# One gate tile moved from the cache stage into the recurrence chain and its outputs, and eight key pages loaded before the cache stage

## The reference, cut to what matters

```python
xn = rms_norm(h); z = xn @ w_in
za, zb, ga, gb = z[..., :c1], z[..., c1:c2], z[..., c2:c3], z[..., c3:]
oa, s_new, _ = rwkv_branch(za, shift0, s0, p)   # a recurrence over time, 8 heads, state 64x64
q, k, v, log_f = fox_features(zb, ...)
ob = attend(q, k, v, log_f)                     # samples: over 2048 cached keys in 16 pages each
merged = sigmoid(ga) * (oa @ proj_a) + sigmoid(gb) * (ob @ proj_b)
h = h + merged @ w_out
h = h + hier_moe(rms_norm(h))                   # 32 experts, two of them for each token
y = rms_norm(h)
```

## Time and profile before

| | us |
|---|---|
| median of 3 runs | 859.84 |
| lowest and highest | 859.52, 865.72 |
| the profiled execution's own time | 862.67 |
| its span, first to last instruction | 861.0 |
| PE busy in the span | 761.1 (88%) |
| DVE busy | 382.5 (44%) |
| ACT busy | 186.4 (22%) |
| POOL busy | 145.3 (17%) |
| mean traffic of the transfers | 254 GB/s |

### The profile page before, as it was taken

The page is one execution under the profiler, slowest core; times in us unless marked ns, Lnnn a source line. Parts: engine busy times, 40 slices in busy tenths (PEclk is TensorE's granted clock), DMA queues, the critical chain, the costliest instruction groups (busy, mean ns, idle before and its releaser), DMA issues. The chain is left out here.

```text
span 861.0 us, 20782 instructions
## 1 busy us (share of the span) xinstructions
PE 761.1 (88%) x8681; PEld 445.5 (52%) x8681; DVE 382.5 (44%) x722; ACT 186.4 (22%) x433; POOL 145.3 (17%) x294
## 2 busy tenths in 40 slices
PE   5999999998989999768898997889889987899985
PEld 2445666675666667624565664455644425444421
DVE  2222623228963174748666774633552222422213
ACT  2101321216332210031422320223111110111103
POOL 8500120007020020031504343422000000000000
PEclk9999999988999989768899998999989998999997
DMA  8721431211332113459899999988939999999993
GB/s 311 284 86 54 190 117 49 97 53 67 103 85 84 32 55 85 105 163 396 364 352 414 397 397 409 362 313 314 422 153 425 421 425 421 426 420 425 421 412 121
DMA packets 54647, 220.26 MB, mean 256 GB/s; under 512 B 21935, under 2 KB 24026, under 8 KB 30746
## 3 DMA queue, kind: packets, MB, share of 16 engines
q1 hardware_dynamic: 46576, 183.28, 54.5%
q0 software_dynamic: 7328, 35.48, 10.7%
q10 hardware_dynamic: 650, 0.18, 0.1%
HBM read 211.82 MB, written 7.09 MB: 254 GB/s over the span
## 5 line engine op out<-in xcount | busy, mean ns | idle before, releaser
L232 PE MATMUL bank<-arena 128*128 128x320 f32 x256 | 85.0, 469 | 3.1 <-DVEq L2200 1.8
L208 POOL DMA_DIRECT2D arena<-in_cv x116 | 59.9, 516 | 113.1 <-PE bank L1897 80.8
L513 PE MATMUL bank<-arena 128*128 128x512 f32 (+1 forms) x144 | 69.9, 624 | 1.4 <-DMA arena<-in_w_zb 1.4
L2508 PE MATMUL bank<-arena 128*32 128x512 f32 x512 | 65.4, 624 | 3.3 <-DMA arena<-in_w_exp 2.1
L2739 DVE TENSOR_TENSOR arena<-arena,bank 128x512 f32<-128x512 f32 x35 | 24.1, 687 | 97.2 <-PE bank L2478 94.2
L548 PE MATMUL bank<-arena 128*128 128x336 f32 x224 | 66.3, 450 | 0.6 <-ACT arena L429 0.6
L1590 DVE STREAM_TRANSPOSE arena<-arena 128x2048 f32<-128x2048 f32 x28 | 63.1, 2288 | 4.3 <-DMA arena<-in_ck 2.9
L232 PEld LDWEIGHTS bank<-arena 128*128 128x128 f32 x256 | 47.5, 199 | 24.8 <-issue 7.6
L1897 PE MATMUL bank<-arena 128*16 128x128 f32 x1024 | 35.6, 300 | 19.7 <-issue 11.4
L548 PEld LDWEIGHTS bank<-arena 128*128 128x128 f32 x224 | 41.5, 189 | 21.4 <-issue 1.7
L1389 ACT ACTIVATE arena<-bank 128x384 f32<-128x384 f32 (+6 forms) x63 | 25.1, 444 | 108.2 <-PE bank L232 31.9
(11 more groups left out here) (495 smaller groups left out, 1103.4 us busy)
## 6 DMA issues: line engine op xcount, KB each, us to landing
arena<-in_w_exp SPq DMA_DIRECT2D x95, 1024.0 KB, 19.1
arena<-in_ck SPq DMA_DIRECT2D x120, 256.0 KB, 6.6
arena<-in_cv POOLq DMA_DIRECT2D x116, 256.0 KB, 7.6
arena<-in_w_gate SPq DMA_DIRECT2D x8, 1024.0 KB, 4.8
arena<-in_w_za SPq DMA_DIRECT2D x7, 1024.0 KB, 6.9
arena<-in_w_zb SPq DMA_DIRECT2D x6, 1024.0 KB, 15.7
arena<-in_w_proj SPq DMA_DIRECT2D x8, 512.0 KB, 9.9
arena<-in_w_out SPq DMA_DIRECT2D x4, 1024.0 KB, 10.6
```

Of the source, the lines that this page charges most:

```text
L208: eng.dma_start(tile[n:P:4, :], src[bass.ds(page, 1)].rearrange("a (p j) n -> (a p) (j n)", j=4))\
L232: mm = nc.tensor.matmul(bank[b][:, 0:TM], w[:, k, a, :], xnT[:, k, NMETA:T], start=(k == 0), stop=(k == KT - 1))
L513: mm = nc.tensor.matmul(bank[q % 6][0:n, :], xnT[:, k, i * P:i * P + n], w[:, k % 4, :], start=(k == 0), stop=(k == KT - 1))
L2508: mm = nc.tensor.matmul(bank[2][j * CAP:(j + 1) * CAP, :], xg[:, q % 2, k, j * CAP:(j + 1) * CAP], place[s][:, (k % 4) * 512:(k % 4 + 1) * ...
```

## The change

It concerns the end of "rwkv_pairs" and the start of "cache".

- `GT_PAIRS` goes from 14 to 15: tile 14 is made in "rwkv_pairs". Its first four slices come after the last two chain steps (`chain_gate` after each of the nine steps now), its last four between the groups of the outputs (after n = 1, 4, 7, 10). It uses bank 3, so the outputs go to banks 0, 1, 2 and 4, and PE waits for the copy of bank 4 first. Only tile 15 is left to "cache".
- SP issues the eight key pages of m = 0, 1 of sequence 1 in "rwkv_pairs", after the suffix sums (L1101) and ahead of the stores of tiles 12, 13 and 14. To make their place free, `cd` and `um` move behind them in memory, and `xl` into `ar`.
- The four transfers of the final state move from the end of "rwkv_pairs" to "cache", behind the projection loads, and with them goes SP's wait there for the stored tiles. The wait for them stands ahead of `key_loads(2)`, as before.
- In "cache" SP takes the four pages of m = 2 from POOL; POOL keeps m = 3.
- On DVE, `turn_keys(1, 0)` stands ahead of the wait for the variance, and `turn_keys(1, 1)` ahead of the reciprocal's wait instead of behind the reciprocal.

```diff
-        GT_PRE, GT_LEVELS, GT_SOLVE, GT_SAMPLES, GT_PAIRS = 6, 9, 11, 12, 14
+        GT_PRE, GT_LEVELS, GT_SOLVE, GT_SAMPLES, GT_PAIRS = 6, 9, 11, 12, 15
...
@@ rwkv_pairs, sync
+                for m in range(2):
+                    load_pages(sp, 11 + m, page_numbers(sp, m, 1), A["ck"])
                 gates_out(GT_SAMPLES, GT_PAIRS)
-                for i in range(2):
-                    sp.wait_ge(S(f"kept_gt{i}"), 16 * (GT_PAIRS // 2))
-                sp.wait_ge(S("w_sp_sb"), 1)
-                for g in range(NPAIR):
-                    sp.dma_start(O["rw_p"][2 * g:2 * g + 2].rearrange("h v k -> v h k"),
-                                 soutp[hs[g % 2], g // 2, :].rearrange("p (h k) -> p h k", h=2)).then_inc(S("kept_rw"), 16)
...
@@ rwkv_pairs, tensor
                     mm.then_inc(S("w_sp"), 1)
-                    if c < 7:
-                        chain_gate(c + 1)
-
+                    chain_gate(c + 1)
+
+                OUT_BANK = (0, 1, 2, 4)
                 pe.wait_ge(S("w_s"), NCH)
-                pe.wait_ge(S("w_gt_sb"), GT_PAIRS - GT_PRE)
+                pe.wait_ge(S("w_o1_sb"), 1)
                 for g in range(NPAIR):
                     for j in range(NT):
...
+                        if (g, j) == (NPAIR - 1, NT - 1):
+                            mm.then_inc(S("w_o"), 1)
+                        n = g * NT + j
+                        if n % 3 == 1:
+                            mm = gate_mm(pe, GT_PAIRS - 1, 3, (4 + n // 3,))
+                            if n // 3 == 3:
+                                mm.then_inc(S("w_gt"), 1)
...
@@ cache, sync
-                for m in range(2):
-                    load_pages(sp, key_slot(1, m), page_numbers(sp, m, 1), A["ck"])
+                for n, page in enumerate(page_numbers(sp, 2, 1)):
+                    page_load(sp, place[key_slot(1, 2)], n, A["ck"], page, S("kept_key2"))
                 proj_load(sp, 0, 0)
                 proj_load(sp, 0, 1)
+                for g in range(NPAIR):
+                    sp.dma_start(O["rw_p"][2 * g:2 * g + 2].rearrange("h v k -> v h k"),
+                                 soutp[hs[g % 2], g // 2, :].rearrange("p (h k) -> p h k", h=2)).then_inc(S("kept_rw"), 16)
                 sp.wait_ge(S("kept_rw"), 16 * NPAIR * (DB + 1))
                 sp.wait_ge(S("ov_ps"), 1)
                 proj_load(sp, 1, 0)
                 key_loads(2)
+                for i in range(2):
+                    sp.wait_ge(S(f"kept_gt{i}"), 16 * ((GT_PAIRS + 1 - i) // 2))
                 sp.wait_ge(S("p_gt_out"), 16 * NPOST)
                 gates_load(0)
...
@@ cache, vector
                 turn_bias(0)
+                turn_keys(1, 0)
                 dve.wait_ge(S("ov_ps"), 1)
                 TS(ovs, bank[7][:, 0:T], 1.0 / HD, GN_EPS, mult, add).then_inc(S("ov_ready"), 1)
-                turn_keys(1, 0)
+                turn_keys(1, 1)
                 dve.wait_ge(S("ort_ready"), 1)
                 nc.vector.reciprocal(ovs, ovs).then_inc(S("ov_rc"), 1)
-                turn_keys(1, 1)
```

More of the change, by code:

```diff
@@ L1039, in build @@
         nn = sp4(NPAIR, 2, NT, CH)
-        cd = sp4(NPAIR, 2, 2, NT, CH)
         mark_bv = sp4.at
@@ L1046, in build @@
         vmm = sv(2, 4, P)
+        assert sp4.at <= odd_at + 2 * SLOT
+        sp4.at = odd_at + 2 * SLOT
+        cd = sp4(NPAIR, 2, 2, NT, CH)
         um = sp4(NPAIR, NT, P)
+        assert sp4.at <= stage[0].offset
         fin = Space(arena, mark_qb, mark_nn)
         soutp = fin(2, P)
+        assert mark_nn > odd_at >= fin.at
         us = [us_a, fin(4, P)]
-        xl = fin(NPAIR, P)
+        xl = ar[:, BE, :, 0:P]
         snew = [Space(arena, mark_nn, mark_nn + DB * HD)(DB, HD), fin(DB, HD)]
@@ L1374, in _ @@
                             for i in range(4):
-                                mm_(bank[i][hs[h], g * 96 + j * CH:g * 96 + (j + 1) * CH], v_tm[strips[i], g, j, hs[h]],
+                                mm_(bank[OUT_BANK[i]][hs[h], g * 96 + j * CH:g * 96 + (j + 1) * CH], v_tm[strips[i], g, j, hs[h]],
                                     cd[strips[i], g, h, 1, j, :], start=True, stop=False)
                             for i in range(4):
-                                mm = mm_(bank[i][hs[h], g * 96 + j * CH:g * 96 + (j + 1) * CH], um[strips[i], g, j, hs[h]],
+                                mm = mm_(bank[OUT_BANK[i]][hs[h], g * 96 + j * CH:g * 96 + (j + 1) * CH], um[strips[i], g, j, hs[h]],
                                          cd[strips[i], g, h, 0, j, :], start=False, stop=True)
-                mm.then_inc(S("w_o"), 1)
-                pe.wait_ge(S("w_o1_sb"), 1)
+                        if (g, j) == (NPAIR - 1, NT - 1):
[5 more added lines that the diff above has]
+                                mm.then_inc(S("w_gt"), 1)
+                pe.wait_ge(S("w_o1_sb"), 2)
                 for q in range(2):
-                    mm = nc.tensor.transpose(bank[4][:, q * P:(q + 1) * P],
+                    mm = nc.tensor.transpose(bank[5][:, q * P:(q + 1) * P],
                                              sbd[:, 2 * q:2 * q + 2, :].rearrange("p g v -> p (g v)"), ident)
@@ L1446, in _ @@
                 gate_out(GT_SOLVE, 7)
-                for j in range(GT_SAMPLES, GT_PAIRS):
-                    gate_out(j, 3)
+                gate_out(GT_SAMPLES, 3)
+                gate_out(GT_SAMPLES + 1, 3)
                 act.wait_ge(S("w_or"), NCH)
@@ L1451, in _ @@
                     cp(ar[:, AL, g, 0:LP], bank[4 + g][:, P:P + LP]).then_inc(S("w_o1_sb"), 1)
+                gate_out(GT_PAIRS - 1, 3)
                 act.wait_ge(S("w_sp_ps"), 1)
-                cp(soutp.rearrange("p q t -> p (q t)"), bank[4][:, 0:2 * P]).then_inc(S("w_sp_sb"), 1)
+                cp(soutp.rearrange("p q t -> p (q t)"), bank[5][:, 0:2 * P]).then_inc(S("w_sp_sb"), 1)
             @block.vector
@@ L1549, in _ @@
                 for i in range(4):
-                    ch(TT(ov[:, :, i, :], ov[:, :, i, :], bank[i][:, 0:384].rearrange("p (a c) -> p a c", c=CH), add))
+                    ch(TT(ov[:, :, i, :], ov[:, :, i, :], bank[(0, 1, 2, 4)[i]][:, 0:384].rearrange("p (a c) -> p a c", c=CH), add))
         retire()
@@ L1783, in _ @@
                 pool.sem_inc(S("hsel_ready"), 1)
[L1784 to L1787, removed]
+                pages = page_numbers(pool, 3, 1)
+                for i in range(2):
+                    pool.wait_ge(S(f"kept_gt{i}"), 16 * ((GT_PAIRS + 1 - i) // 2))
+                for n in range(4):
+                    page_load(nc.gpsimd, place[key_slot(1, 3)], n, A["ck"], pages[n], S("kept_key3"))
                 for g in range(NPAIR):
```

## The result

The changed kernel is slower. In 20 runs its median is 868.18 us (861.72 to 876.96), that of the kernel before, run beside it, 864.1 (854.08 to 878.6). The ratio is **1.0068, interval 1.0037 to 1.0099**: 5.9 us lost by 865, where the forecast was 8.0 won. The profiled execution took 868.66 us, its span is 867.1: 6.0 more than the profile of before. Disturbed executions, more than 1.5% above the fastest of the same kernel, are left out of the ratios and the readings, and the profiles of changed_again, changed_gates_early and before_again were such.

A forecast was written before the change was run, and what follows sets the result against it. PE, DVE and ACT handing work on in series, transfers close behind, were taken to bound the kernel; 0 (block start) + 8.0 (first fills earlier) = 8.0 won, 859.84 - 8.0 = 851.8 us, range 848 to 858.

The forecast's parts named there:

- Chain's end and outputs: End of the recurrence block: added gate slices leave the cache block's start unchanged, from 1 earlier to 4 us later.
- the term of 0.5: Outputs: four gate slices cost 0.5 us, mostly covered by PE's 3.6 us wait for issue; ends 0 and 5.6.
- DVE at the head: Cache block's head: earlier key turns start the maxima 4.2 us earlier and let `scores(1)` meet its keys 7.3 earlier.
- SP, with the moved stores: Cache block: state stores issued by 384.4 land 5 us later; `key_loads(2)` begins 1.5 late at 392.4, ends +0 and +19.
- The gates' landing: Cache block: gates' load issued at 406.7 instead of 410.76, the sigmoid beginning 5 to 6.6 us after it.
- the gap at 410 to 415: Cache block: idle transfer time there, 1.6 us, closes and counts toward transfers being about 7 us ahead.
- Sigmoid to `scores(2)`: Cache block: exponentials 3.76 us after the sigmoid, DVE takes fill output 3.9 later, then three fills at 2.6 each.
- one for one: Whole kernel: what is won before 630 us comes out at the end in full.
- the slower side: Rival, cache block: SP stands at state stores landing in 10.1 to 23.2 us, delaying keys, gates and fills; chance 0.07.
- Only the transfers count: Rival, whole cache block: only saved transfers matter, 3.5 to 5 us won, 855 to 856; chance 0.17.
- the outputs pay: Rival, outputs: four slices lie bare at the low clock, 5.6 us, block starts 4 later, 856; chance 0.11.
- the change does not do what it says: Rival: pages asked for in the chain block land only in the cache block; about 3 us won, 857; chance 0.04.

The follow-up runs named there:

- changed_again: The changed kernel run a second time, nothing altered, against the kernel before: ratio 1.0066 (1.0031 to 1.0102).
- changed_gates_early: The changed kernel, stores where the change puts them, with the first gates' load issued behind the pages of m = 1 of `key_loads(2)`: ratio to before 0.9959 (0.9925 to 0.9993).
- before_again: The kernel before, unchanged, timed against itself: ratio 0.9983 (0.9946 to 1.002).
- tile_alone: The kernel before with only the gate tile's move (tile 14 in the last chain steps and outputs): ratio to before 1.0002 (0.9972 to 1.0032).
- changed_third: The changed kernel run a third time, nothing altered, against the kernel before: ratio 1.0028 (0.998 to 1.0076).
- stores_first: The changed kernel with the four state stores as SP's first transfers of the cache block: ratio to before 0.9936, and 0.9933 the second time.
- stores_back: The changed kernel with the four state stores back at the end of "rwkv_pairs", behind the tiles' stores: ratio to before 0.994 (0.9906 to 0.9975).
- keys_ahead_of_wait: The changed kernel with `key_loads(2)` issued ahead of SP's wait for the state stores: ratio to before 0.9985 (0.9953 to 1.0017).
- stores_alone: The kernel before with only the state stores moved behind `proj_load(sp, 0, 1)`, and SP's wait for the state gone: ratio to before 1.0041 (1.0006 to 1.0076).

## Why the prediction was wrong

In the profile the changed kernel was 14.0 us from the forecast (8.0 won forecast, 6.0 lost). Two steps failed: SP's stand at the moved stores, and the landing time of the gates' load behind it. By its own steps:

- **Ahead of the change**, 2.6: chance, as shown. It is part of this profile, not of the 1.0068.
- **Chain's end and outputs**, taken at 0 with ends -1 and 4: 2.6 in this profile, 0.6 behind the eighth step, as forecast, and 2.0 from the ninth step to the block. Over ten profiles with the tile in the outputs, these take 11.3 to 13.7 us (mean 12.6), in three without it 10.5, 10.6 and 11.4. The group rows of the changed kernel (355 to 378 us) show why:

```profile
L232 PE MATMUL bank<-arena 128*128 128x320 f32 x16 | 6.5, 513 | 0.0
L1375 PE MATMUL bank<-arena 32*64 32x32 f32 x192 | 5.2, 238 | 4.3 <-issue 4.3
```

  The sixteen are four after the eighth step, four after the ninth (1.34 us each four) and eight in the outputs: 6.5 - 2 x 1.34 = 3.8 us for those. The wait for issue did not close over them as I argued: it was 4.3 us here, against 3.6 before, and 1.8 in tile_alone, where it closed in part. By the means, the term of 0.5 was too small by 1.2 and within its ends.
- **DVE at the head**: right. Maxima at +17.0 after the first matmul, +17.9 forecast; tile 15 done at +21.2, +23.1 forecast; keys of `scores(1)` at +25.5, +26.4 forecast. The wait for value pages at `weigh(0)` went, as forecast. PE reached the end of `weigh(0)` at +41.3 instead of +38.0: the key products took 6.97 us at a clock of 0.52, behind 400 to 405, in which PE was busy for 2.35 us, and 1.83 went to issue.
- **SP, with the moved stores**: the step that failed first. I took them as issued at +10.9 after the first matmul, and 5 us more for their landing ("3.4 + 2 us: 5 us, near the lower end"), though the case's own rows had 10.1 for the projection loads of that queue. They were issued at +12.7, mostly since the four took 4.01 us to issue and not 2.7, and SP then stood 6.7 us; from issue to landing they took 7.8, and 9.0 in changed_third, where SP stood 8.1. `key_loads(2)` came at +22.2 where +18.9 was forecast, and the gates' load at +36.7 where +33.2 was: 3.5 late. stores_first, stores_back and keys_ahead_of_wait take this delay away, and all end at or below the time of before.
- **The gates' landing**: the larger term, and no rival had it. I took 5 to 6.6 us from the one row of before. It was 10.0 and 11.6 in the changed kernel, and 9.4 to 11.9 in every other kernel whose sigmoid waited for it. Before, 410 to 415 had a transfer share of 0.68, since SP had just stood 5.8 us for tile 15's store: the load met a queue that had gone partly dry. I counted that gap among the gains ("the gap at 410 to 415 (0.32 of 5 us is 1.6) and part of the one before it close") and kept the landing time that stood beside it. That the gap made it possible is argued: no run closes the gap alone, and the profile of before_again, left out above, has the gap too (a share of 0.65) and 8.6 us, so chance may have part of the 6.6. Against 5.8, the middle, it is 4.2 late.
- **Sigmoid to `scores(2)`**: 16.5 us, 15.5 by the forecast: 1.0.

The sum: 2.6 + 2.6 + 3.5 + 4.2 + 1.0 = 13.9. Up to `scores(7)` and to the end the distance to the kernel before stays what it was there (565.13 - 558.98 = 6.15, and 867.1 - 861.0 = 6.1): **one for one** was right.

Of the rivals, the slower side had the right mechanism: SP stands at the state stores, and keys, gates and fills follow. It had 0.07, and its price was too high for the landing (10.1 to 23.2, the win "gone when the stores land 13 us after issue") and too low for what follows. By its own rule a landing of 7.8 would have left 5 us of gain; with the gates' later landing and the later start of the block all of it was gone. What the argument against it said, that the 23.2 us load stood behind 6 MB, is beside the point: 3 MB made 7.8. "Only the transfers count" and "the outputs pay" would have left the kernel faster, and "the change does not do what it says" is out: the pages had landed.

**What stays open.** The two profiles of the changed kernel have `scores(2)` 2.6 and 3.4 us later after the ninth step than before, 3.2 and 4.0 with the slices behind the eighth; the ratios 1.0068, 1.0066 and 1.0028 say 5.9, 5.7 and 2.4. Much of the loss lies in that stretch, but up to 3 us of it aren't placed. The third ratio alone doesn't tell the loss from none. Repeats of one kernel differ by up to 0.7% (1.0066 and 1.0028; 0.9959 and 0.9887), so effects of 3 us are told apart only between kernels that ran side by side, if there.

## What to carry to other kernels

A small transfer for which an issuing engine later waits belongs ahead of the large ones, or on a queue that is idle: behind 3 MB, four stores of 32 KB held all later loads up, and the transfers ran dry meanwhile. When a change removes a wait, ask what that wait was covering and which load profited from the idle queue behind it; the landing time read in such a gap may not hold once the gap is closed (6.6 us became 9.4 to 11.9 here). And before a transfer is called late, look for the earliest point at which its own inputs allow it: moving the gates' load up by eight pages gave about as much as moving the stores, 1.1 to 1.4% against 1.3%. Take one wait away, and look for the next: behind the gates stood the late keys.

## What the runs showed of the hardware

- Four stores of 32 KB landed in 2.0 us as the first of their queue (stores_first), in 7.7 to 9.0 behind 3 or 4 MB of pages and projection loads (stores_alone, changed_third); with SP standing for them, traffic fell from 383 GB/s at 390 to 395 to 60 in the next window.
- One load of 1280 KB landed in 6.6 us in a window with a transfer share of 0.68 (8.6 in before_again, with 0.65) and in 9.4 to 11.9 with the share at 0.90 or more.
- The granted clock of one stretch of one program, 310 to 320 us, PE busy 10.00 of 10 us, was 0.50 (the 1.2 GHz level throughout) in one execution and 0.89 in another, and what followed lay 4.5 us apart (356.63 and 352.09).
- Runs of 32x32 matmuls stopped for issue 3.6 to 4.5 us in all without larger slices between them, and 1.8 to 4.3 with four; nothing in these profiles says why the sum differs from one execution to the next.
- In these outputs the granted clock was 0.50, the 1.2 GHz level, in the three profiles without the slices and 0.70 to 0.88 in the ten with them. PE was busy for 6.9 us there without and 9.4 to 10.6 with them: the slices of 3.8 us added 2.5 in the changed kernel.
